# A two-layer decoder step: sample states and head sums in array quarters, first gather moved ahead

## The chip, the cores and the metric

One core of a Trainium2 chip runs the whole kernel; the other cores are not used. The metric is the device time of one execution in microseconds, lower is better, given as the median of several runs.

## What is computed

One inference step of a two-layer decoder, for a prompt of 256 tokens and 8 samples of 4 tokens, so 288 token columns, with D = 1024, all in fp32. Layer 0 is sparse attention beside a short convolution and a dense feed-forward block. Layer 1 is RWKV-7 time mixing with 16 heads of 64, and then a mixture of 8 experts of which each token takes 2. The change touches only layer 1. Three parts of it matter here:

```python
kk = heads(k * k_k)
kk = kk * lax.rsqrt(jnp.maximum(jnp.sum(kk * kk, axis=-1, keepdims=True), 1e-24))   # per token and head

def step(S, inp):                      # S: 64 x 64 per head; output wkv_sample is S after the 4 tokens
    r_t, w_t, k_t, v_t, kk_t, a_t = inp
    sa = jnp.einsum('bhvk,bhk->bhv', S, -kk_t)
    S = S * w_t[:, :, None, :] + sa[..., None] * (kk_t * a_t)[:, :, None, :] + v_t[..., None] * k_t[:, :, None, :]
    return S, jnp.einsum('bhvk,bhk->bhv', S, r_t)

for e in range(N_EXPERTS):             # top-2 of 8, combine holds the two gates of a token
    out = out + combine[..., e:e + 1] * swiglu(x, w_gate[e], w_up[e], w_down[e])
```

The per-head sum of squares over 64 channels, its inverse root, and that factor laid back over the 64 channels of each head are the "head sums" and the "spreading". The "new states of the sample" are the 16 heads x 8 samples of S after the 4 tokens.

## The kernel before, in words

The five engines run five instruction streams written by hand, tied by semaphores; the order of work is the order of the code in each stream. SP (SyncE) issues nearly all loads of weights and most of the outputs. A matmul in fp32 is two instructions on TensorE, and each has its weight load, so counts in the profile are twice those of the code. The channels of a token lie on partitions, 128 to a chunk, eight chunks (index c or hp), two heads to a chunk (index par, partitions 0 to 63 and 64 to 127).

**Time mixing, the factors.** TensorE runs 48 projection jobs of 16 instructions (`krv_job`, through the helper on line 774), each [128 x 128] weights against 288 columns. Between them stand small jobs. After job 32 it waits for ScalarE's squares `sqk` and sums them by head (line 1156): eight accumulating matmuls with a [128 x 16] slice of the constant `head_rows`, one per chunk, into 16 partitions of bank 0. Then jobs 33 to 35, during which VectorE clamps the sums (line 2353), ScalarE takes the root (line 1864), VectorE inverts and negates (lines 2355, 2356); GpSimd forms the decayed keys at the same time (lines 2883, 2884), and waits for the sums too before it does. Then TensorE spreads the 16 rows `rn` over all channels (line 1165): eight matmuls with [16 x 128] slices of `spread16`, into six banks in turn, so that the seventh and eighth wait for VectorE's products of line 2359 to free a bank. Then jobs 36 to 38, then the cross products of line 1175, which wait for VectorE's lines 2359 to 2367. `spread16` is laid out once by GpSimd (line 2871) behind the copies of the last rows. VectorE's stream before that: the token mixes (line 2327, in sets of eight), two small vectors (2332, 2333), the decay scale, the running sums and exponentials, the factor `kf` (line 2345), on which GpSimd waits to start its products of line 2877 and 2878, one pair per chunk as projections come. ScalarE squares them four chunks at a time.

**New states of the sample.** For each chunk hp, `new_state(hp)` on TensorE waits until GpSimd has decayed the old state `Ss`, and then turns the eight samples' 64 x 64 blocks with the identity, for both heads (line 1461, 16 matmuls, so 32 instructions), and adds `Zs` times `BKm`, 512 columns per head (line 1465, 4 instructions). Head par reads partitions of half par, and writes half par of its own bank (`K_BANKS[hp][par]`). ScalarE copies each head's half of 64 x 512 back to `Ss` (line 1982), and SP writes it out with one transfer per head (line 716). States 0 to 3 are made during the group norm of the mixing output, state 4 after the router's logits are turned, states 5, 6 and 7 after the rank sums (line 1554) that place each token in its experts. States 6 and 7 use the banks of states 4 and 5 and wait for their copies.

On ScalarE, `new_state(1)` stands between the squares of the group norm (line 1970) and its root (line 1976), on which VectorE (2549) and GpSimd (2922) wait, and then TensorE's transposes of y (1482).

**Experts.** `Ss` lies in the memory of the third of three weight buffers (`part2`, over the old ring). SP loads 16 pieces of 704 KB (gate and up of expert 0) ahead, then makes sure that all new states have been written out (`ws_out`), reads the number of blocks, and enters a loop with the pieces from 16 on: each waits until TensorE has used the piece that it replaces. A block is at most 96 tokens for each expert. TensorE reads the number of blocks, waits for the copy of state 7, and enters its loop: `gather()` picks the block's tokens of expert 0 by matmul (line 1573, 72 instructions into banks 0 and 1), VectorE turns them into `xe` (2649) and applies the gain (2654), then the eight experts follow: gate, up, gate (line 1607, columns in four quarters of the array), down (1624), up, the gather of the next expert, down. After the last expert it scatters the block (1591). Gate uses banks 0 to 2, up 3 to 5, down 6 and 7. The selection in `pick` for expert 0 is made by VectorE (2642) right after the ranks and before the rest of its preamble, which ends at line 2765.

**Names.** `half_(i)` is partitions 64i to 64i+63. `turned_s(engine, name)` waits for the copies of that name. `bk[i]` is PSUM bank i, 128 partitions x 512 columns.

## Time and profile before

| | |
|---|---|
| Median of 3 runs | 1519.91 us |
| Lowest, highest | 1518.69, 1524.91 us |
| The profiled execution's own time | 1520.28 us |
| Its span in the trace | 1518.5 us |
| TensorE matmul busy | 1451.0 us, 96% |
| VectorE, ScalarE, GpSimd busy | 457.5, 223.0, 165.6 us |
| HBM traffic | 375.59 MB read, 6.73 MB written, 252 GB/s over the span |
| Time-mixing layer | about 470 to 768 us |
| Router, states 4 to 7, gather | about 768 to 788 us |
| Experts | 787.8 to about 1503 us |

Times inside the trace count from the start of the span; between the span and the execution's own time lie 1.8 us. The span is the same whatever an engine's share of busy time is, so the chain of waits tells more than the shares. On the chain, "issue" is time in which the engine waited for nothing that the profile shows. PEclk in the windows is the granted TensorE clock as a share of 2.4 GHz.

### The profile page before, as it was taken

What the parts mean: (1) busy time and instruction counts of PE and PEld (TensorE: products, weight loads), DVE (VectorE), ACT (ScalarE), POOL (GpSimd) and SP (SyncE); (2) the same over time, 40 slices, a digit from 0 to 9 for tenths busy, and PEclk for the clock granted to TensorE, in tenths of its full rate; (3) what the DMA queues carried; (4) which work ended last, traced back from release to release, by engine and by line L of the source; (5) the groups of instructions that cost most, each with busy time, mean ns of one, the idle gap of its engine ahead of it and who ended that gap; (6) DMA issues with size and microseconds to landing.
All of it is one profiled execution on the core that took longest, in us unless ns stands there. A gap on an engine that the chain in (4) does not pass through costs nothing.

```text
span 1518.5 us, 39153 instructions
## 1 busy us (share of the span) xinstructions
PE 1451.0 (96%) x17792; PEld 936.8 (62%) x17792; DVE 457.5 (30%) x983; ACT 223.0 (15%) x485; POOL 165.6 (11%) x208
## 2 busy tenths in 40 slices
PE   6989989999999999987989999999999999999996
PEld 4767877777777777776644545555454555545453
DVE  2399331111024557774331110212111021211123
ACT  3144120000003412233120000000000000000001
POOL 4237200000000315125100000000000000000100
PEclk9999999999999999998999999999999999999999
DMA  9745034444534420305579999999999999999995
GB/s 287 219 139 153 14 113 145 133 135 143 162 104 116 132 84 3 59 3 143 191 276 414 413 411 412 374 413 369 414 385 396 414 369 413 373 412 386 394 403 217
DMA packets 187551, 384.86 MB, mean 253 GB/s; under 512 B 42463, under 2 KB 125631, under 8 KB 187258
## 3 DMA queue, kind: packets, MB, share of 16 engines
q1 hardware_dynamic: 180352, 365.84, 65.5%
q0 software_dynamic: 3616, 12.85, 2.2%
q10 hardware_dynamic: 3418, 3.68, 0.7%
q8 instruction: 140, 2.29, 0.6%
q14 instruction: 25, 0.20, 0.0%
HBM read 375.59 MB, written 6.73 MB: 252 GB/s over the span
## 4 chain that ended last, share of the span: by engine, by line
PE 88%; DVE 8%; DMA 1%; ACT 1%; issue 1%; SPq 0%; POOL 0%; DVEq 0%; ACTq 0%
PE bk L1607 30%; PE bk L1624 15%; PE bk L1089 11%; PE bk L774 9%; PE bk L1102 6%; PE bk L1526 2%; PE bk L1573 2%; PE bk L1004 2%; PE bk L1195 1%; DMA ring<-in_w_in_even 1%; DVE left L2184 1%; DVE tops L2182 1%; PE bk L1117 1%; PE bk L1138 1%; DVE sc_p L2169 1%
## 5 line engine op out<-in xcount | busy, mean ns | idle before, releaser
L1607 PE MATMUL bk<-part,xe 128*32 128x352 f32 x6144 | 459.1, 460 | 2.3 <-DVE xe L2654 2.3
L1607 PEld LDWEIGHTS bk<-part,xe 128*32 128x32 f32 x6144 | 207.8, 110 | 248.3 <-issue 245.9
L1624 PE MATMUL bk<-part,hidT 128*32 128x256 f32 x4224 | 231.4, 379 | 1.2 <-DVE hidT L2693 1.2
L1624 PEld LDWEIGHTS bk<-part,hidT 128*32 128x32 f32 x4224 | 141.9, 110 | 88.7 <-issue 2.6
L2689 DVE TENSOR_TENSOR hp<-sg,bk 128x352 f32<-128x352 f32 x48 | 37.6, 784 | 468.1 <-PE bk L1607 468.1
L1089 PE MATMUL bk<-xn,ring 128*128 128x288 f32 x704 | 173.8, 410 | 3.3 <-DMA ring<-in_ffn_up 3.3
L1089 PEld LDWEIGHTS bk<-xn,ring 128*128 128x128 f32 x704 | 135.4, 192 | 41.3 <-issue 3.5
L774 PE MATMUL bk<-mx,ring 128*128 128x288 f32 x384 | 98.1, 415 | 0.0
L774 PE MATMUL bk<-xg,ring 128*128 128x288 f32 x336 | 88.3, 422 | 8.2 <-DMA ring<-in_w_in_even 6.6
L774 PEld LDWEIGHTS bk<-mx,ring 128*128 128x128 f32 x384 | 73.2, 193 | 21.4 <-issue 1.2
L1102 PE MATMUL bk<-hid,ring 128*128 128x288 f32 x352 | 85.5, 406 | 0.0
L774 PEld LDWEIGHTS bk<-xg,ring 128*128 128x128 f32 x336 | 65.2, 197 | 27.7 <-issue 7.3
L1102 PEld LDWEIGHTS bk<-hid,ring 128*128 128x128 f32 x352 | 66.9, 190 | 18.5
L2942 POOL TENSOR_TENSOR free_now<-row_ss 128x1 f32 x5 | 1.0, 193 | 668.2 <-DMA expert_rows<-ye 650.3
L2042 ACT COPY ye<-bk 32x256 f32<-32x256 f32 x48 | 17.4, 363 | 368.4 <-PE bk L1624 367.8
L2035 ACT ACTIVATE sg<-bk 128x352 f32<-128x352 f32 x48 | 22.3, 464 | 313.3 <-PE bk L1607 309.3
L2716 DVE COPY ye<-bk 32x256 f32<-32x256 f32 x48 | 20.3, 422 | 99.0 <-PE bk L1624 98.3
L2268 DVE TENSOR_TENSOR gs<-bk,rs 128x288 f32<-128x288 f32 x22 | 10.1, 458 | 128.6 <-PE bk L1089 128.6
L1526 PE MATMUL bk<-gT,ro 128*128 128x288 f32 x128 | 34.5, 427 | 0.0
L2864 POOL MEMSET rmask<- 128x288 f32 x1 | 0.5, 496 | 311.4 <-DVE xg L2276 311.4
L1573 PE MATMUL bk<-xr,pick 128*32 128x256 f32 x576 | 32.6, 379 | 1.5 <-ACT Ss L1982 1.5
L1813 ACT ACTIVATE sg<-gs 128x288 f32<-128x288 f32 x22 | 9.8, 444 | 151.9 <-DVE gs L2268 151.9
(535 smaller groups left out, 1298.3 us busy)
## 6 DMA issues: line engine op xcount, KB each, us to landing
part<-in_moe_gate SPq DMA_DIRECT2D x136, 704.0 KB, 7.2
part<-in_moe_up SPq DMA_DIRECT2D x136, 704.0 KB, 8.6
part<-in_moe_down SPq DMA_DIRECT2D x128, 704.0 KB, 8.5
ring<-in_rwkv_w_rkv SPq DMA_DIRECT2D x24, 512.0 KB, 4.0
ring<-in_ffn_gate SPq DMA_DIRECT2D x22, 512.0 KB, 6.0
ring<-in_ffn_up SPq DMA_DIRECT2D x22, 512.0 KB, 5.2
ring<-in_ffn_down SPq DMA_DIRECT2D x22, 512.0 KB, 4.6
ring<-in_w_in_even SPq DMA_DIRECT2D x16, 512.0 KB, 6.9
```

Of the source, the lines that this page charges most:

```text
L774: last = mm(out, w[:, k], rhs[:, k], start=k == 0, stop=k == KC - 1)
L1004: last = nc.tensor.matmul(bk[4 + c // 2][:, TP * (c % 2):TP * (c % 2) + TP], w[:, k], mixT[:, k, 0:TP], start=k == 0 and c % 2 == 0, stop= ...
L1089: last = mm(bk[2 * m + f % 2][:, 0:T], slots[2 * m + k // 4][:, k % 4, (f % 2) * P:(f % 2 + 1) * P], xn1[:, k], start=k == 0, stop=k == KC ...
L1102: last = mm(bk[banks[c]][:, 0:T], w[:, f % 2, c * P:(c + 1) * P], hid[:, f], start=f == 0, stop=f == FC - 1)
L1526: last = mm(bk[OUT_BANK(c)][:, 0:T], w[:, k], gT[:, k], start=k == 0, stop=k == KC - 1)
L1573: last = mm(gate_bk[g // 2][32 * q:32 * q + 32, 256 * (g % 2):256 * (g % 2) + 256], pick[:, i, 32 * g:32 * g + 32], in_parts[:, q], start= ...
L1607: last = mm(banks[g][32 * c:32 * c + 32, 0:FQ], xe[:, k, 32 * g:32 * g + 32], parts[ph % 3][:, FH * k + FQ * c:FH * k + FQ * c + FQ], star ...
L1624: last = mm(down_bk[g // 2][32 * q:32 * q + 32, 256 * (g % 2):256 * (g % 2) + 256], hidT[:, half, g, 32 * m:32 * m + 32], parts[ph % 3][:, ...
L2035: nc.scalar.activation(sg2[:, g], gate_bk[g][:, 0:FQ], ACT.Silu).then_inc(silu_ok, 1)
L2042: last = nc.scalar.copy(ye[32 * g:32 * g + 32, 256 * q:256 * q + 256], down_bk[g // 2][32 * q:32 * q + 32, 256 * (g % 2):256 * (g % 2) + 256])
L2689: V.tensor_tensor(hp[:, g].rearrange("p (m j) -> p j m", m=NM), sg2[:, g].rearrange("p (j m) -> p j m", m=NM), up_bk[g][:, 0:FQ].rearrange ...
L2716: last = V.tensor_copy(ye[32 * g:32 * g + 32, 256 * q:256 * q + 256], down_bk[g // 2][32 * q:32 * q + 32, 256 * (g % 2):256 * (g % 2) + 256])
```

## The change

Three things are done.

1. **Head sums and spreading.** The sums of chunks 0 to 3 go to four column quarters of the array (32 columns each, partitions 32(c%4) and up of bank 0), and chunks 4 to 7 accumulate into the same four. `head_rows` is 34 wide, and its slice of 32 puts the two heads of a chunk on rows 12 and 13 (c < 4) or 14 and 15 of the quarter. `rn` has 128 rows. The spreading reads the quarter's 32 rows with a new table `head_of`, made by VectorE in four copies behind the mixes of set 4; GpSimd's `spread16` is gone.
2. **New states in four quarters.** Even samples are written to half par and odd ones to the other half; bank `K_BANKS[hp][0]` holds the even ones of both heads and `K_BANKS[hp][1]` the odd ones, 256 columns each. The wide product becomes four of 256 columns. ScalarE copies 128 x 256 per bank. SP writes four transfers of 64 KB per state.
3. **The first gather.** TensorE reads the block count after state 5, gathers, makes states 6 and 7, and enters the loop. The gather that opened the loop's body now closes it. The wait for state 7's copy stands before the first up product.

```diff
-    c["head_rows"] = np.arange(30)[None, :] == 14 + (p // HD)[:, None]
+    c["head_rows"] = np.arange(34)[None, :] == 14 + (p // HD)[:, None]
...
-    rn = sbt("rn", [RH, T], at=starts["rs"])
-    spread16 = sbt("spread16", [RH, D], at=starts["cst"] + 4 * COL["sin"][0])
+    rn = sbt("rn", [P, T], at=starts["rs"])
+    head_of = sbt("head_of", [P, 2, 2, HD], at=starts["cst"] + 4 * COL["sin"][0])
+    quarter = lambda c: slice(32 * (c % 4), 32 * (c % 4) + 32)
+    HALF_NB = NB // 2 * HD
...
             turned_s(sp, f"K{hp}")
+            by_parity = O["wkv_sample"][0].rearrange("(j o) h v k -> o h v j k", o=2)
             for par in range(2):
-                sp.dma_start(O["wkv_sample"][0, :, 2 * hp + par].rearrange("b v k -> v b k"),
-                             Ss[half_(par), hp].rearrange("p (b k) -> p b k", b=NB)).then_inc(ws_out, 16)
+                for odd in range(2):
+                    rows = Ss[half_(par ^ odd), hp, HALF_NB * odd:HALF_NB * odd + HALF_NB]
+                    sp.dma_start(by_parity[odd, 2 * hp + par], rows.rearrange("p (j k) -> p j k", k=HD)).then_inc(ws_out, 16)
...
-        sp.wait_ge(ws_out, 16 * RH)
+        sp.wait_ge(ws_out, 32 * RH)
...
-            last = mm(bk[0][0:RH, 0:T], C["head_rows"][:, 14 - 2 * c:30 - 2 * c], sqk[:, c], start=c == 0, stop=c == KC - 1)
+            at = 2 - 2 * (c // 4)
+            last = mm(bk[0][quarter(c), 0:T], C["head_rows"][:, at:at + 32], sqk[:, c], start=c < 4, stop=c >= 4)
...
-            mm(bk[c % 6][:, 0:T], spread16[:, P * c:P * c + P], rn[:],
+            mm(bk[c % 6][:, 0:T], head_of[quarter(c), c // 4].rearrange("p a v -> p (a v)"), rn[quarter(c)],
...
             for b in range(NB):
+                odd, at = b % 2, b // 2 * HD
                 for par in range(2):
                     r = half_(par)
-                    mm(bk[K_BANKS[hp][par]][r, b * HD:(b + 1) * HD], Ss[r, hp, HD * b:HD * b + HD], C["ident64"][r],
-                       start=b == 0, stop=False, skip_group_check=True)
-            for par in range(2):
-                r = half_(par)
-                last = mm(bk[K_BANKS[hp][par]][r, :], Zs[r, hp], BKm[r, hp].rearrange("p b k -> p (b k)"),
-                          start=False, stop=True, skip_group_check=True)
+                    mm(bk[K_BANKS[hp][odd]][half_(par ^ odd), at:at + HD], Ss[r, hp, HD * b:HD * b + HD], C["ident64"][r],
+                       start=b < 2, stop=False, skip_group_check=True)
+            for odd in range(2):
+                for par in range(2):
+                    r = half_(par)
+                    last = mm(bk[K_BANKS[hp][odd]][half_(par ^ odd), 0:HALF_NB], Zs[r, hp],
+                              BKm[r, hp].rearrange("p (j o) k -> p o j k", o=2)[:, odd],
+                              start=False, stop=True, skip_group_check=True)
...
         new_state(5)
-        for hp in (6, 7):
-            turned_s(pe, f"K{hp - 2}")
-            new_state(hp)
...
                 if k == 0 and e == 0:
+                    turned_s(pe, "K7")
                     pe.wait_ge(sc_ok, blk * 6 + 6)
...
-        turned_s(pe, "K7")
         pe.wait_ge(lg_mm, KC + 1)
+        pe.wait_ge(pick_ok, 1)
+        gather()
+        for hp in (6, 7):
+            turned_s(pe, f"K{hp - 2}")
+            new_state(hp)
         with pe.Fori(0, n_blocks) as blk:
-            pe.wait_ge(pick_ok, blk * NE + 1)
-            gather()
             for e in range(NE):
                 expert(blk, e)
             for g in range(6):
                 scatter(blk, g)
+            gather()
...
-            for par in range(2):
-                last = nc.scalar.copy(Ss[half_(par), hp], bk[K_BANKS[hp][par]][half_(par), :])
+            for odd in range(2):
+                last = nc.scalar.copy(Ss[:, hp, HALF_NB * odd:HALF_NB * odd + HALF_NB], bk[K_BANKS[hp][odd]][:, 0:HALF_NB])
...
         mixed(4, 0)
+        for c in range(4):
+            r = quarter(c)
+            V.tensor_copy(head_of[r].rearrange("p h a v -> p (h a) v"),
+                          C["ident"][r, 32 * c + 12:32 * c + 16].unsqueeze(2).broadcast_to([32, 4, HD]))
...
-        V.tensor_scalar(rn[:], bk[0][0:RH, 0:T], 1.0e-24, None, ALU.max).then_inc(nk_ok, 1)
+        V.tensor_scalar(rn[:], bk[0][:, 0:T], 1.0e-24, None, ALU.max).then_inc(nk_ok, 1)
...
-        G_.tensor_copy(spread16[:].rearrange("p (h v) -> p h v", h=RH),
-                       C["ident"][0:RH, 0:RH].unsqueeze(2).broadcast_to([RH, RH, HD])).then_inc(mask_ok, 1)
```

## Rows read from the trace of the kernel before

**Rows 1.** The page's part 4, the chain that ended last, by engine

```profile
PE 88%; DVE 8%; DMA 1%; ACT 1%; issue 1%; SPq 0%; POOL 0%; DVEq 0%; ACTq 0%
```

**Rows 2.** The chain in order of time (start us, us, what), time-mixing layer

```profile
535.01 3.98 PE bk L1156 x16
539.00 11.84 PE bk L774 x48
550.84 5.56 PE bk L1165 x16
556.40 13.68 PE bk L774 x48
```

**Rows 3.** Windows (busy us and instructions by engine, PEclk, DMA share, GB/s)

```profile
535.00:539.00 4.00, 4.00 (x18) 1.48 (x17) 0.47 (x2) 1.73 (x3) 0.00 (x0) 1.00 0.44 131
...
553.30:556.30 3.00, 3.00 (x7) 1.66 (x5) 1.52 (x4) 0.00 (x0) 0.00 (x0) 0.50 0.19 55
556.40:560.10 3.70, 3.70 (x8) 2.70 (x9) 3.63 (x4) 0.00 (x0) 0.00 (x0) 0.50 0.00 0
...
788.90:792.20 3.30, 3.30 (x28) 1.21 (x24) 0.00 (x0) 0.00 (x0) 0.00 (x0) 0.50 1.00 415
```

**Rows 4.** The chain in order of time, state 5 and experts

```profile
774.18 1.08 PE bk L1461 x32
775.26 0.86 PE bk L1465 x4
...
787.78 44.50 PE bk L1607 x576
```

**Rows 5.** Timeline (start, us, engine, line, operation, [idle before <-releaser])

```profile
717.22 1.17 ACT L1982 COPY Ss<-bk 64x512 f32<-64x512 f32 x2
...
779.80 0.14 DVE L2765 COPY blocks_f<-blocks_f 1x1 f32<-1x1 f32 x1
779.99 1.17 ACT L1982 COPY Ss<-bk 64x512 f32<-64x512 f32 x2 [0.86 <-PE bk L1465]
...
781.39 3.62 PEld L1573 LDWEIGHTS bk<-xr,pick 128*32 128x32 f32 x72 [2.33 <-issue]
...
785.55 1.11 DVE L2649 STREAM_TRANSPOSE xe<-bk 128x256 f32<-128x256 f32 x3 [5.60 <-PE bk L1573]
```

**Rows 6.** Timeline of VectorE, time-mixing layer

```profile
541.97 2.53 DVE L2356 TENSOR_SCALAR rn<-rn 16x288 f32<-16x288 f32 x1
...
551.55 2.46 DVE L2359 TENSOR_TENSOR t<-t,bk 128x288 f32<-128x288 f32 x5 [7.05 <-PE bk L1165]
...
556.93 2.29 DVE L2362 TENSOR_TENSOR AR<-t,cumx 128x2048 f32<-128x2048 f32 x1
...
562.40 2.29 DVE L2367 TENSOR_TENSOR BK<-aT,cum 128x2048 f32<-128x2048 f32 x1
```

**Rows 7.** Groups by form on TensorE (busy us, mean ns, idle before)

```profile
L1573 PE MATMUL bk<-xr,pick 128*32 128x256 f32 x576 | 32.6, 379 | 1.5 <-ACT Ss L1982 1.5
...
L1015 PE MATMUL bk<-sc,cst 32*128 32x256 f32 x16 | 1.4, 426 | 0.0
```

**Rows 8.** Timeline of GpSimd, factors

```profile
523.91 1.00 POOL L2877 TENSOR_SCALAR t<-kT,vecT 128x288 f32<-128x288 f32 x1 [0.25 <-ACT kT L1838]
```

**Rows 9.** Groups by form on ScalarE, 530 to 790

```profile
L1919 ACT COPY BKs<-bk 64x256 f32<-64x256 f32 x4 | 1.5, 365 | 0.3 <-PE bk L1227 0.3
```

**Rows 10.** Timeline of TensorE, level products

```profile
580.04 1.16 PE L1195 MATMUL bk<-Y,Cj 64*64 64x64 f32 x64 [1.84 <-DVE Y L2385]
```

**Rows 11.** The line of the output transfers (ns min/median/max, first and last start)

```profile
L716 SPq DMA_DIRECT2D out_wkv_sample<-Ss x16: 595/632/1308, 715.6 to 781.8; - x16
```

**Rows 12.** DMA issues by line (KB each, median us to landing)

```profile
out_wkv_sample<-Ss SPq DMA_DIRECT2D x16, 128.0 KB, 2.5
```

**Rows 13.** Timeline of SP, first experts

```profile
785.34 3.94 SPq L736 DMA_DIRECT2D part<-in_moe_gate  x8
```

**Rows 14.** Timeline of TensorE, the end

```profile
1503.00 4.63 PE L1591 MATMUL bk<-ye,giveT 96*32 96x512 f32 x36 [1.49 <-DVE ye L2716]
```

More of the change, by code:

```diff
@@ L296, in build @@
     rmask = sbt("rmask", [P, T], at=starts["cst"] + 4 * COL["cos"][0])
-    rn = sbt("rn", [RH, T], at=starts["rs"])
-    spread16 = sbt("spread16", [RH, D], at=starts["cst"] + 4 * COL["sin"][0])
-    assert COL["sin"][0] + D <= COL["delta_mask"][0]
+    rn = sbt("rn", [P, T], at=starts["rs"])
+    head_of = sbt("head_of", [P, 2, 2, HD], at=starts["cst"] + 4 * COL["sin"][0])
+    assert COL["sin"][0] + 4 * HD <= COL["delta_mask"][0]
+    quarter = lambda c: slice(32 * (c % 4), 32 * (c % 4) + 32)
     Sp = sbt("Sp", [P, 2, KC, HD])
@@ L1160, in _ @@
         pe.wait_ge(rn_ok, 1)
-        pe.wait_ge(mask_ok, 2)
         for c in range(KC):
```

## The prediction, made before the kernel was run

> **What bounds the kernel now.** I read the page's chain first: almost nine tenths of the span is TensorE work [rows 1], so an edit pays only where it shortens TensorE's own queue or removes what that queue waits for. Then I read the chain in order of time at the two places that the diff touches. In the time-mixing layer it runs on TensorE without a break through the head sums, 48 projection matmuls, the spreading and 48 more projection matmuls [rows 2]; nothing else is late there. Two things stand out. The head sums and the spreading are single matmuls one after another over 16 columns or 16 rows of the array. And the second 48 projection matmuls take 13.68 us where the first 48 take 11.84: the windows show why, a granted clock of 0.50 (1.2 of 2.4 GHz) from about 553.3 to 560.1 us, which began while TensorE was in the spreading [rows 3]. The head sums before it left the clock at full speed. At the second place the chain goes through states 5, 6 and 7, then the gather, then the first expert [rows 4, 5]; between them TensorE stands idle twice, first for ScalarE's copy of state 7, then, from 785.5 to 787.78, for VectorE's transposes of the gathered columns [rows 5]. Another half-speed stretch lies right behind that second pause, 788.9 to 792.2 [rows 3]. From there on the expert stage is TensorE at a fixed pace to the end.
>
> **Head sums.** Before: 16 instructions (two per fp32 matmul), 3.98 us [rows 2], 0.25 us each. After: the same number, but eight matmuls with 32 columns each in four column quarters. The nearest row is the expert product, also 128x32 in four column quarters, 576 in 44.50 us [rows 4], 77 ns each for 352 moving columns; for 288 that is 63 ns, so 16 take 1.0, with the last one's drain 1.1 us. Gain 2.9 (bounds: 0 if the quarters don't overlap, 3.0). The 32-row result costs the engines behind it nothing new: they work per partition on the same 288 columns. Their answer now comes 2.9 earlier; before it was ready at 544.5 (VectorE's last step, stretched to 2.53 us [rows 6]) and was used at 550.8, so over 6 us of projections cover it before and after.
>
> **Spreading.** Before: 5.56 us [rows 2], of which 3.0 at half clock. After: each matmul has 32 rows and 128 columns, four row quarters at once into four banks. The nearest row is the selection's spreading, the same 32x128 form in four row quarters and four banks: 16 instructions of 256 columns busy for 1.4 us [rows 7]; one after another at 0.25 x 256/288 each they would be 3.6, so they overlap. The first four matmuls then take about 0.6 us. Six banks serve eight results, so matmuls 6 and 7 wait for VectorE's products 0 and 1, 0.49 us apiece [rows 6]: first product at +0.7, second done at +1.7, last matmul done at +2.3. Gain 5.56-2.3 = 3.3 (bounds: 1.6 if nothing overlaps but the clock stays up, 4.7 if VectorE held nothing back). VectorE becomes the slower one here: eight products end at +4.6, that is at 547.9+4.6 = 552.5 instead of 556.9. Its following work took from 556.93 to 564.69 [rows 6], so it is done at 560.3. The matmuls that need it come after 48 projections: 547.9+2.3+11.84 = 562.0. So TensorE stays the bound with 1.7 us in hand; if that is gone, VectorE's chain is late next.
>
> **The clock there.** The array read 16 of 128 rows for the stretch before the clock fell. After the change the quarters read all 128 and the light stretch is 2.3 us with projections on both sides, so I take the fall as gone: the 48 projections run 11.84 instead of 13.68, gain 1.8 (bounds 0 and 1.8). The first part of the layer gives 2.9+3.3+1.8 = 8.0 us.
>
> **What pays for it.** VectorE gets four copies of 32x256 behind the second set of mixes. A product of 288 elements a partition takes it 0.49 us [rows 6], so they are 2.0 at most, and exponentials, factors and GpSimd's products start that much later. GpSimd already waits 0.25 us for ScalarE's copy of a projection before its sixth pair at 523.91 [rows 8], and each pair takes 1.8 where a projection takes 3.9, so it has caught up a pair later, some 7 us before the head sums. I cost it at nothing; without that cover it is 2.0. GpSimd loses its one copy, off the path: nothing.
>
> **States 0 to 3** lie in the group norm, where TensorE waits. ScalarE's two copies of state 1 (1.17 us, 64x512 [rows 5]) stand between the squares and the root of the path. They become two of 128x256; a 256-column copy takes 0.365 [rows 9], so 0.73: gain 0.4 (bounds 0.4 and -1.3: TensorE finishes these states sooner, idles longer, and its clock could fall before the transposes of y).
>
> **States 4 to 7 and the gather.** A state now costs 1.08+0.86 = 1.94 us [rows 4]: 32 instructions on two of the four 64x64 quarters, then four of 512 columns. After: the 32 go round all four; 64 such instructions take 1.16 us on four quarters [rows 10], so 0.6; the wide products become eight of 256 columns over four, half of 0.86 plus a drain, 0.5. About 1.1 a state. The order becomes: state 5, the read of the block count, gather, states 6 and 7, loop. State 5 starts at 774.18 as before (it follows the rank sums, which wait for ScalarE) and ends at 775.3. The read of the count was under ScalarE's copy before and is bare now; the trace does not show it alone. It is between nothing and the 2.3 us from TensorE's last weight load to the gather's first [rows 5]; I take 0.9, since that gap also held the copy's second half and its signal. Gather at 776.2, 4.16 us until VectorE takes it, then 2.23 until the expert starts, as before [rows 4, 5]: 782.6. TensorE's states 6 and 7 end at 780.4+2.2 = 782.6, entering the loop adds perhaps 0.3. VectorE's own preamble ended at 779.94 [rows 5], so it is there in time, or 0.6 late if entering its loop costs it a microsecond. Expert 0 starts at 783.1 against 787.78: gain 4.7 (bounds 3.3 and 5.6). The wait for state 7's copy now stands before the second product of expert 0, 14 us later: nothing.
>
> With the idle 2.3 us gone I take the half-speed stretch behind it as gone too: half of 3.3 us [rows 3], gain 1.7 (bounds 0 and 1.7).
>
> **Queues and the end.** SP issues 16 output transfers for these four states instead of eight, and weights 16 and up wait for all. At 0.63 us per issue [rows 11] state 7's four go out from 783.5 to 786; they land 2.5 later, weights from about 789 instead of 785.34 [rows 12, 13]. Expert 0 first needs them after two thirds of the 44.50 us row, 783.1+29.7 = 812.8. Slack shrinks by 8 us and stays above 15: nothing. The loop's closing gather runs once for no one, as the 576 instructions of rows 7 are eight gathers of 72, so one block; it starts when TensorE's last work ends, 1507.6 [rows 14], and takes 4.1 (8.2 at half clock), with the span going on to 1518.5: nothing.
>
> **Sum:** 8.0+0.4+4.7+1.7 = 14.8 us off the profiled execution's 1520.3 is 1505.5. The median of the three runs shown is 0.4 below that execution; I leave the forecast at 1505.5. A measurement here tells about 0.5% (7.6 us) from no change.
>
> **Rivals.** (a) The clock gives nothing: both stretches stay, or others appear, since what precedes each shifts by some us. 1505.5+1.8+1.7 = 1509. For: the work before the first expert still has two short pauses. Against: the head sums did not bring it down. 0.20. (b) VectorE or a bare wait is late next: its chain misses 562.0 by a few us, or count read and loop entry take the full 2.3: together up to 5 us, 1510. 0.12. (c) The state products don't overlap fourfold, because both row halves now write the same bank at once, where before each had its own. Then states 6 and 7 stay 1.94 each, the expert starts at 784.6, and the time is 1507. Against: the level products of rows 10 are on four quarters with both row halves in one bank, and take 18 ns each against 34 for the state's. 0.05. The Trainium skill (TensorEngine Tiling (Array Packing), Gotcha 1: PSUM Pressure) says row tiles can't access one bank simultaneously; by that rule (c) would hold, and the trace's row disagrees. (d) Quarters don't overlap in the head sums and the spreading and the clock still falls: that part gives nothing, 1513.5, no change. Against: rows 4 and 7. 0.05. (e) Slower: the outputs' transfers hold up the weights. If each of the 16 costs SP D us, the loads start at 775+16D+2.5 and land 4 later; TensorE stalls once D exceeds 2.0, and the time passes 1528 once D exceeds 3.4, since a stalled expert stage regains nothing. Against: 0.63 per issue now. 0.03. The Trainium skill (DMA: Bandwidth & Descriptors, Rules for kernel authors) has transfers below 64 KB pay mostly overhead; these go from 128 KB [rows 12] to 64, and no row of before shows one of that size here.
>
> **Chances.** Forecast 0.55, its own range 1502 to 1508.5. Faster by over 0.5% (below 1512.3): 0.55+0.20+0.12+0.05, less what of (b) spills over, 0.90. Same 0.07, slower 0.03. The range 1501.5 to 1512.5 takes in (a) to (c) and a clock that rises elsewhere.
>
> **What would show it.** Head sums near 1.1 us, spreading near 2.3, clock 1.00 through 545 to 562, the cross products at 562; a state's 32 instructions in 0.6 us; the gather near 768 and expert 0 near 775 on the shifted axis; no SP wait in the expert stage that TensorE has to wait for. Wrong if TensorE waits for VectorE before the cross products, or if a half-speed stretch stands at a new place on the chain.

## The result and the profile after

| | before | after |
|---|---|---|
| Median | 1521.20 us (4 runs) | 1512.01 us (4 runs) |
| Lowest to highest | 1518.69 to 1524.91 | 1510.52 to 1516.85 |
| Profiled execution, its span | 1520.28, 1518.5 | 1516.85, 1515.0 |

The ratio is 0.9941, with a 95% interval from 0.9924 to 0.9958: 9.2 us faster, where 14.8 were forecast. The profiled execution of after was its slowest of four, so its span hides part of the gain, and I ran the same kernel again below (`changed_again`) for a second trace.

Line numbers below the edits move: L1156 is now L1161, L1165 is L1170, L774 is L778, L1461 is L1467, L1573 is L1578, L1607 is L1612, L716 is L721.

The page's part 4 (the chain by engine) and part 2 (the granted clock in 40 slices) of after, against [rows 1]:

```profile
PEclk9899999999999999998899999999999999999999
...
PE 88%; DVE 8%; DMA 1%; issue 1%; ACT 1%; SPq 0%; DVEq 0%
```

The bound is the same. The page alone doesn't show the change: the places have to be read one by one. The chain in order of time, against [rows 2]:

```profile
539.20 1.11 PE bk L1161 x16
540.30 11.84 PE bk L778 x48
552.14 0.73 PE bk L1170 x8
552.87 0.45 DVE t L2372
553.32 0.04 issue
553.36 1.11 PE bk L1170 x4
554.47 11.84 PE bk L778 x48
566.31 2.02 PE bk L1180 x128
...
578.73 1.99 PE bk L1200 x64
580.72 6.05 PE bk L778 x16
586.77 2.02 PE bk L1200 x128
588.79 4.08 PE bk L778 x16
```

From the head sums to the cross products it takes 566.31 - 539.20 = 27.1 us; in [rows 2] it is 535.01 to 570.08, 35.1. The one step on VectorE is the wait of matmul 6 for its bank. But two things are new: the head sums start 4.2 us later than before, in front of which no work was changed on TensorE; and 12 us behind the cross products, 64 level products take 1.99 us where [rows 10] has 1.16, and 16 projection instructions take 6.05 where the next 16 take 4.08. The windows of after (columns as in [rows 3]) name the cause, and two more such places:

```profile
578.20:585.00 6.80, 6.27 (x74) 4.95 (x75) 6.68 (x8) 1.45 (x3) 0.00 (x0) 0.52 0.01 2
...
721.60:731.80 10.20, 10.20 (x32) 6.63 (x33) 8.07 (x19) 1.50 (x3) 5.66 (x6) 0.52 0.32 66
776.00:783.00 7.00, 6.19 (x65) 3.32 (x65) 4.28 (x37) 1.46 (x6) 0.00 (x0) 0.53 0.38 78
```

The granted clock is about half (1.2 of 2.4 GHz) at each. The second stretch begins behind the pause before the transposes of y, the third in the new gather. The timeline of the second place in the changed kernel, columns as in [rows 5], shows the group norm:

```profile
716.78 0.65 PE L1472 MATMUL bk<-BKm,Zs 64*64 64x256 f32 x8
717.44 0.63 ACT L1991 COPY Ss<-bk 128x256 f32<-128x256 f32 x2
...
718.55 1.90 POOL L2934 TENSOR_TENSOR y_rows<-y_rows,gst 128x1024 f32<-128x1024 f32 x1 [6.48 <-DVE gst L2562]
...
721.11 0.39 PE L1490 MATMUL bk<-cst,y_rows 128*128 128x128 f32 x1 [3.68 <-DVE y_rows L2567]
```

ScalarE's copies of state 1 take 0.63 us where two of [rows 5] took 1.17, and TensorE stands still for 3.68 us behind state 3, where it stood still for 2.35 us before. And TensorE's timeline at the gather, against [rows 4, 5]:

```profile
774.90 0.69 PE L1467 MATMUL bk<-cst,Ss 64*64 64x64 f32 x32
775.42 0.71 PE L1472 MATMUL bk<-BKm,Zs 64*64 64x256 f32 x8
776.93 6.88 PE L1578 MATMUL bk<-xr,pick 128*32 128x256 f32 x72 [0.81 <-DVE pick L2655]
783.75 0.69 PE L1467 MATMUL bk<-cst,Ss 64*64 64x64 f32 x32
784.26 0.61 PE L1472 MATMUL bk<-BKm,Zs 64*64 64x256 f32 x8
784.70 0.64 PE L1467 MATMUL bk<-cst,Ss 64*64 64x64 f32 x32
785.16 0.61 PE L1472 MATMUL bk<-BKm,Zs 64*64 64x256 f32 x8
786.12 4.32 PE L1612 MATMUL bk<-part,xe 128*32 128x352 f32 x53 [0.35 <-DVE xe L2667]
```

States 6 and 7 now lie under VectorE's transposes, and the two idle pauses are gone but for 0.81 and 0.35 us. The gather itself takes 6.9 us instead of 4.13.

The next table cuts the span of each trace at the same seven places, to show where the time went. The stretches are cut at the first instruction of a line on TensorE; in brackets stands the time lost to a low clock, (1 - PEclk) times the length of the window, in us. For the first expert to the scatter, 715 us long, PEclk is rounded to 1.00 in each; the 1.7 is from the half-speed stretch of 3.3 us in [rows 3].

| stretch | before | after | changed_again |
|---|---|---|---|
| start to head sums | 534.9 | 539.1 | 535.7 |
| head sums to cross products | 35.1 (3.5) | 27.1 (0) | 27.1 (0) |
| cross products to transposes of y | 151.6 (4.5) | 154.9 (10.8) | 153.7 (9.2) |
| transposes of y | 5.5 (1.6) | 6.9 (3.4) | 6.7 (3.1) |
| output projection to rank sums | 45.6 (1.8) | 45.5 (1.8) | 45.7 (1.8) |
| rank sums to first expert | 15.1 (0) | 12.6 (3.4) | 11.0 (1.8) |
| first expert to scatter | 715.2 (1.7) | 713.5 (0) | 713.5 (0) |
| scatter to end | 15.5 | 15.4 | 15.4 |

So 8.0 came from the head sums, 2.5 to 4.1 from the path to the experts, 1.7 behind the first expert; 3.3 (or 2.1) and 1.4 (or 1.2) were given back in the two middle stretches, and 4.2 (or 0.8) ahead of the change. The runs had to tell what of this is the change's doing.

### The profile page after: what moved, and what is told of

Read it like the earlier page. It is cut to its first block, busy times and chain, and to the rows that moved or that the text cites. A ratio compares the mean times of both kernels' runs of the same rounds, so it can differ in the third digit from the quotient of the medians.

```text
span 1515.0 us, 39378 instructions
## 1 busy us (share of the span) xinstructions
PE 1451.6 (96%) x17896; PEld 940.7 (62%) x17896; DVE 456.6 (30%) x987; ACT 218.7 (14%) x485; POOL 164.2 (11%) x207
## 3 DMA queue, kind: packets, MB, share of 16 engines
q10 hardware_dynamic: 3418, 3.68, 0.7%
## 4 chain that ended last, share of the span: by engine, by line
PE 88%; DVE 8%; DMA 1%; issue 1%; ACT 1%; SPq 0%; DVEq 0%
PE bk L1612 30%; PE bk L1629 15%; PE bk L1093 11%; PE bk L778 9%; PE bk L1106 6%; PE bk L1578 2%; PE bk L1534 2%; PE bk L1008 2%; PE bk L1200 1%; DMA ring<-in_w_in_even 1%; DVE left L2193 1%; DVE tops L2191 1%; PE bk L1121 1%; PE bk L1142 1%; DVE sc_p L2178 1%
## 5 line engine op out<-in xcount | busy, mean ns | idle before, releaser
L1612 PE MATMUL bk<-part,xe 128*32 128x352 f32 x6144 | 457.4, 459 | 0.3 <-DVE xe L2667 0.3
L1612 PEld LDWEIGHTS bk<-part,xe 128*32 128x32 f32 x6144 | 207.3, 110 | 245.1 <-issue 242.7
L778 PE MATMUL bk<-xg,ring 128*128 128x288 f32 x336 | 90.3, 429 | 9.0 <-DMA ring<-in_w_in_even 8.9
L778 PE MATMUL bk<-mx,ring 128*128 128x288 f32 x384 | 98.2, 415 | 0.0
L778 PEld LDWEIGHTS bk<-mx,ring 128*128 128x128 f32 x384 | 73.2, 193 | 21.2 <-issue 0.9
L778 PEld LDWEIGHTS bk<-xg,ring 128*128 128x128 f32 x336 | 66.7, 201 | 29.0 <-issue 9.6
L1578 PE MATMUL bk<-xr,pick 128*32 128x256 f32 x648 | 40.3, 400 | 0.8 <-DVE pick L2655 0.8
L1578 PEld LDWEIGHTS bk<-xr,pick 128*32 128x32 f32 x648 | 23.5, 116 | 17.0 <-issue 6.2
## 6 DMA issues: line engine op xcount, KB each, us to landing
part<-in_moe_down SPq DMA_DIRECT2D x128, 704.0 KB, 14.8
```

Source lines behind the costliest of these rows:

```text
L778: last = mm(out, w[:, k], rhs[:, k], start=k == 0, stop=k == KC - 1)
L1578: last = mm(gate_bk[g // 2][32 * q:32 * q + 32, 256 * (g % 2):256 * (g % 2) + 256], pick[:, i, 32 * g:32 * g + 32], in_parts[:, q], start= ...
L1612: last = mm(banks[g][32 * c:32 * c + 32, 0:FQ], xe[:, k, 32 * g:32 * g + 32], parts[ph % 3][:, FH * k + FQ * c:FH * k + FQ * c + FQ], star ...
```

## The experiments

Twelve runs, in three rounds. Beside each round the kernel before was run too: medians 1521.88 (27 runs), 1523.31 (17) and 1520.95 us (11). Ratios are to it.

### One part at a time

`heads_only`, `states_only` and `gather_only` are the kernel before with one numbered part of the change each; their diffs are the hunks of `head_rows`/`rn`/`head_of`, of `new_state`, and of `gather()` with `turned_s(pe, "K7")`, as printed above.

> Head sums and spreading in quarters alone, on the kernel before. Clock theory (each part saves the work that was forecast, and part of it is given back because TensorE idles between smaller pieces and its clock falls at new places): the stretch from the head sums to the cross products is 27.1 us as in the changed kernel instead of 35.1, and a fall of the clock in the level products costs 0 to 3: 5 to 8 us faster than before. Rival (the parts' gains overlap, and the 9 us come from this part alone): 9 us faster. Rival (the gain of this part is swallowed by VectorE's chain further on): under 3 us faster.

Measured: 1518.08 us, ratio 0.9970 [0.9954, 0.9985]. The chain:

```profile
538.02 1.11 PE bk L1158 x16
...
565.14 2.02 PE bk L1177 x128
```

27.1 us again, 8.0 less than before, but the median gained only 3.8 us, less than the 5 to 8 expected. The stretch starts at 538.0, 3.1 later than before, much as in after (more on that below), and where it is 33.5 in the old code the gain is 6.4 (`gather_only`).

> New states in four quarters alone, on the kernel before. Clock theory: a state's 32 instructions in 0.56 us and its wide ones in 0.5, the path from state 5 to the first expert 13.6 us before becomes about 10.4 (three states shorter by 0.85, the last copy by 0.5), and the group norm gives 0.5; with a clock fall at the first expert as before, 3 us faster; with a new one in the router or the gather, 0 to 2. Rival (SP's 32 transfers delay the expert weights): TensorE waits for pieces of the third buffer in expert 0.

Measured: 1519.87 us, 0.9989 [0.9975, 1.0003]. From the rank sums to the first expert 13.3 us instead of 15.1, and the two pauses remain. The clock fell while TensorE made states 5 and 6: their 32 instructions took 1.14 and 1.09 us there, those of state 7 at full clock 0.65. The transposes of y take 6.2 (2.5 lost to the clock) instead of 5.5. Behind the first expert there is no half-speed stretch (713.5 us to the scatter), although the order of gather and states is the old one.

> First gather ahead of states 6 and 7 alone, on the kernel before. Clock theory: states still 1.9 us each, so states 6 and 7 take 3.9 us behind the gather and end 1.7 us after the gathered columns are ready: the path from state 5 to the first expert becomes about 10.8 us instead of 13.6, 2.8 faster at full clock, 0 to 1 faster if the clock falls in the gather. Rival (the closing gather costs time at the end): the span behind the last scatter is longer than before by up to 4 us.

Measured: 1517.06 us, 0.9969 [0.9956, 0.9982]. The median is 4.8 us below the kernel before's, where 2.8 were expected. From the rank sums to the first expert 11.1 us, at full clock, with the old states of 1.94 us each. That is as short as in `changed_again`, which lost 1.8 us to the clock there. That chain ends so:

```profile
785.56 0.86 PE bk L1465 x4
786.42 42.74 PE bk L1604 x576
```

VectorE has `xe` ready at 785.60, and TensorE starts the expert 0.8 us later, when it is through with state 7. In the full change `xe` ends last (785.99, and the expert starts at 786.12). So the quartering does shorten this path, by some 0.6 us at full clock (10.5 in `fill_both` below), and the clock, which fell on this path in nearly all traces of quartered states, took that back. The first expert's half-speed stretch is gone in this kernel too (713.5). But it is also missing in `before_wide` below, which is the kernel before with one wider table:

```profile
790.60:1504.10 713.50, 710.76 (x10875) 366.46 (x10876) 109.23 (x204) 38.55 (x94) 6.62 (x11) 1.00 0.99 397
```

Of the four traces with the old order it stands in two (before and `heads_only`, 715.2) and not in the other two (`before_wide` and `states_only`). So the 1.7 us of the table are not shown to be the change's doing. The first stretch of `gather_only` is of old code only:

```profile
535.00 3.98 PE bk L1156 x16
538.99 11.84 PE bk L774 x48
550.83 4.07 PE bk L1165 x16
554.90 13.53 PE bk L774 x48
```

The spreading took 4.07 here and 5.56 in [rows 2]: in that code the clock falls each time (all four traces with it), but not at the same moment, so this stretch is 33.5 or about 35. In before and `states_only` it fell inside the spreading. In `gather_only` and `before_wide` it stayed up through the spreading and fell about 1 us behind it (in `gather_only` 0.99 from 554 to 556 us and 0.50 from 556 to 559), and less time was lost. Measured from 33.5 the gain of the new code is 6.4. The windows of the next stretch, cross products to transposes of y, follow for three kernels, none of which changes a line on TensorE there, one fence per kernel: before, `gather_only`, `heads_only`.

```profile
570.00:721.60 151.60, 131.85 (x3754) 111.61 (x3753) 100.75 (x166) 48.28 (x96) 53.48 (x39) 0.97 0.23 52
```

```profile
568.40:724.00 155.60, 136.28 (x3753) 115.42 (x3752) 100.72 (x166) 48.18 (x96) 53.51 (x39) 0.93 0.23 51
```

```profile
565.10:716.70 151.60, 130.06 (x3753) 110.16 (x3753) 100.68 (x166) 48.19 (x96) 53.47 (x39) 0.98 0.23 52
```

151.6 us at a clock of 0.97 or 0.98, 155.6 at 0.93: the length of this stretch goes with the clock of the execution, and it is long and short in old code alike. The execution that my sum was made against was one of the short ones. The product of the three ratios is 0.9928; the whole change has 0.9941 and 0.9947. No interaction shows beyond the intervals.

### Is the idle time what the clock answers to?

A filler is a matmul of the identity against `xT` into a bank that is free, whose result nothing reads. It does no work of the kernel; it only keeps TensorE running in a pause.

`fill_levels`: in front of the first level products, where TensorE waits for VectorE twice, 1.84 and 1.30 us, between 574.4 and 578.7 in after. The added wait is for a result that is long there, and keeps the filler behind the last use of its bank.

```diff
             for p2 in range(2):
+                if j == 1:
+                    pe.wait_ge(job_ok, NIN + 39)
+                    fill(6, 3 - p2)
                 pe.wait_ge(y_ok, 2 * (j - 1) + p2 + 1)
```

> The changed kernel with idle matmuls in the two pauses in front of the first level products only (three and two, 128x128 against 288 columns). Clock theory: no half-speed stretch in the level products, 1.5 to 3 us faster than the changed kernel in the median. Rival: as the changed kernel, 1512, or up to 0.5 slower for the fillers.

Measured: 1509.93 us, 0.9917 [0.9890, 0.9944]. The stretch took 151.2 us, 3.0 lost to the clock.

`fill_both` adds two fillers behind state 4 and one before the gather.

```diff
         new_state(4)
+        fill(7, 2)
         pe.wait_ge(sel2_ok, 1)
...
         pe.wait_ge(lg_mm, KC + 1)
+        fill(2, 1)
         pe.wait_ge(pick_ok, 1)
```

> The changed kernel with idle matmuls of 128x128 against 288 columns, whose results nothing reads, in TensorE's pauses: three and two in front of the first two level products, two in front of the rank sums, one in front of the first gather. Clock theory: the clock stays at 1.00 through the level products and the gather; level products and the projection behind them 2.8 us shorter, gather 4.2 instead of 6.9, so 4 to 6 us faster than the changed kernel where its clock fell at both. Rival (the clock has no part in it): no faster than the changed kernel, or slower by what the fillers outlast the pauses (up to 1 us).

Measured: 1510.07 us, 0.9923 [0.9903, 0.9943]. 152.1 us in the middle stretch, 7.6 lost. From the rank sums to the first expert 10.5, with no fall:

```profile
768.00:795.00 27.00, 25.12 (x422) 13.33 (x424) 11.66 (x72) 9.21 (x23) 1.60 (x2) 1.00 0.43 129
```

These are shorter than after's, but 151.2 and 152.1 lie at or near the short end of what unfilled kernels showed (151.6 to 155.6), so the lengths alone don't show what the fillers did. `all_gaps` below tells more by place. At the gather the clock does tell. In the nine other traces with quartered states the clock fell between the rank sums and the first expert (1.7 to 3.4 us lost), whether or not the gather had been moved; in the four with the old states it did not. This is the only kernel with quartered states in which it stayed at 1.00 there, and its gather took 4.1 us. It is one trace, and it gained little time: kernels with the change and without these fillers needed 10.5 to 12.6 us for this path. The fillers themselves cost some: the gather starts 3.8 us behind the first rank sum, and 3.3 in `changed_again`.

`fill_y` fills the pause before the transposes of y with five matmuls.

```diff
         turned_s(pe, "K0")
         new_state(3)
+        turned_s(pe, "K1")
+        fill(4, 5)
```

> The changed kernel with five idle matmuls behind state 3, in TensorE's pause before the transposes of y. Clock theory: with the quartered states TensorE ends them sooner, idles longer, and its clock falls one stretch earlier; with the pause filled the transposes run at full clock, from the first transpose of y to the first output projection 4.5 to 5 us instead of 6.5 to 6.9, and the half-speed stretch behind it is shorter or gone, up to 5 us in all. Rival (the transposes wait for VectorE and ScalarE, and the clock is set by what they themselves keep busy): 6.5 to 6.9 us as before, and the half-speed stretch stays.

Measured: 1509.95 us, 0.9937 [0.9920, 0.9954]. The window of the transposes, of `fill_y` first and then of `changed_again`, which ran on the same chip:

```profile
717.80:722.60 4.80, 4.58 (x24) 3.02 (x25) 3.84 (x8) 1.18 (x3) 1.82 (x3) 1.00 0.48 100
```

```profile
716.50:723.20 6.70, 6.70 (x25) 4.09 (x26) 4.91 (x10) 1.11 (x3) 2.54 (x4) 0.53 0.48 99
```

4.8 us at clock 1.00 against 6.7 at 0.53, and the output projection behind it 44.9 instead of 45.7. The fall goes with the pause. Filled, in `fill_y` and in `all_gaps`, it is gone; in every profile with quartered states and an empty pause of 3.5 to 4.0 us it is there (6.2 to 6.9 us), and with the old, longer states and a pause of 1.3 to 2.4 us it is milder (5.2 to 5.6). The output projection alone says less (it took 44.7 to 46.1 in kernels without this filler), but the two stretches together, from the transposes to the rank sums, took 49.6 and 49.7 us with it and 50.9 to 52.5 in the twelve other traces.

`states_in_gaps` uses real work instead: state 5 goes before the rank sums and state 6 ahead of the gather.

```diff
         new_state(4)
+        new_state(5)
         pe.wait_ge(sel2_ok, 1)
...
-        new_state(5)
+        turned_s(pe, "K4")
+        new_state(6)
...
-        for hp in (6, 7):
-            turned_s(pe, f"K{hp - 2}")
-            new_state(hp)
+        turned_s(pe, "K5")
+        new_state(7)
```

> The changed kernel with the same states at other places: state 5 in front of the rank sums, state 6 in front of the gather, state 7 alone behind it, so that TensorE's two pauses there hold work. Clock theory: no fall of the clock in the gather, which takes 4.2 us instead of 6.9; first expert 2 to 3 us nearer to the rank sums than in the changed kernel, 2 to 3 us faster in the median. Rival (the clock has no part, the gather waits for the picks): no faster, since the picks and the transposes set the time either way.

Measured: 1510.3 us, 0.9912 [0.9886, 0.9939]. From the rank sums to the first expert 11.0 us, 1.8 lost to the clock, as in `changed_again` without the move: a miss. The states in the pauses did not keep the clock up, and the interval overlaps the change's own.

### The late start of the head sums

Kernels with the new head sums start them at 535.7 to 542.0 us, with the old ones at 534.9 to 536.3. The change makes the table of constants four columns wider (`head_rows`), and that table is loaded at the start. `same_width` takes the four columns off another constant in the changed kernel, `before_wide` gives the kernel before the wider one.

```diff
-    c["slots"] = np.tile(np.arange(P)[None], (P, 1))
+    c["slots"] = np.tile(np.arange(P - 4)[None], (P, 1))
```

```diff
-    c["head_rows"] = np.arange(30)[None, :] == 14 + (p // HD)[:, None]
+    c["head_rows"] = np.arange(34)[None, :] == 14 + (p // HD)[:, None]
```

> The changed kernel with the last constant four columns narrower (its last four are never read), so that the table of constants is 2942 wide again and every tile behind it lies where it lay in the kernel before. In the three profiles of kernels with the wider table the head sums start at 538.0 to 542.0 us, in the three with the old width at 534.9 to 536.3. Layout theory (the 16 bytes more per row, or the 32-byte shift of the tiles, slow the first loads): head sums start at 535 to 537 and the median is 3 us below the changed kernel's, some 1509. Rival (chance: the first loads vary by themselves): head sums anywhere from 534 to 542, median as the changed kernel's, about 1512.

> The kernel before with head_rows 34 columns wide instead of 30, nothing else: the opposite edit. Layout theory: 3 us slower than before, head sums start at 538 or later. Rival (chance): no difference from before within 1.5 us.

Measured: `same_width` 1512.36 us, 0.9917 [0.9893, 0.9941], head sums at 540.1; `before_wide` 1524.24 us, 1.0002 [0.9987, 1.0017], head sums at 535.7. The width is not it. The traces say where the time lies, though not why. The first matmul of line 1008 (1004 before), in layer 0, starts at 164.3 us in before and at 168.5 in after, and from there to the head sums it takes 370.6 us in both. In the fourteen traces that first matmul starts between 164.3 and 171.4 us, and the rest takes 369.5 to 370.8. So all of the lateness arises ahead of that matmul and of every changed instruction (VectorE's four copies start at 504.67 in after), and those copies cost the path nothing. What varies there is open. `before_wide` also gave a third trace of old code in the middle stretch, nearly as slow as `gather_only`:

```profile
569.20:724.20 155.00, 136.44 (x3753) 115.55 (x3752) 100.88 (x166) 48.20 (x96) 53.47 (x39) 0.93 0.23 51
```

### Rows or length: what brought the clock down in the spreading

The old spreading differs from the new in two ways: it reads 16 rows of the array, and it runs 4 to 5.6 us instead of 2.3. `spread_128_rows` is the changed kernel with the eight matmuls one after another again, but over all 128 rows.

```diff
-    head_of = sbt("head_of", [P, 2, 2, HD], at=starts["cst"] + 4 * COL["sin"][0])
+    head_of = sbt("head_of", [P, KC, 2, HD], at=starts["cst"] + 4 * COL["sin"][0])
...
-            mm(bk[c % 6][:, 0:T], head_of[quarter(c), c // 4].rearrange("p a v -> p (a v)"), rn[quarter(c)],
+            mm(bk[c % 6][:, 0:T], head_of[:, c].rearrange("p a v -> p (a v)"), rn[:],
...
-        for c in range(4):
-            r = quarter(c)
-            V.tensor_copy(head_of[r].rearrange("p h a v -> p (h a) v"),
-                          C["ident"][r, 32 * c + 12:32 * c + 16].unsqueeze(2).broadcast_to([32, 4, HD]))
+        for c in range(KC):
+            row = 32 * (c % 4) + 12 + 2 * (c // 4)
+            V.tensor_copy(head_of[:, c], C["ident"][:, row:row + 2].unsqueeze(2).broadcast_to([P, 2, HD]))
```

> The changed kernel, but the spreading reads all 128 rows in eight matmuls one after another, with a table that is zero outside a chunk's two rows, instead of 32 rows in quarters. Rows theory (the old spreading let the clock fall because it read 16 of 128 rows, not because of its length): 16 instructions at 0.24 us, 3.9 to 4.3 us instead of 2.3, at full clock, and the projections behind it 11.8: head sums to cross products 28.8 to 29.2, 1.7 to 2 us slower than the changed kernel. Rival (its length, 4 us of matmuls with K small in number, let it fall): the clock falls in it, 33.5 to 35.1 less the 2.9 of the sums, so 30.6 or more.

Measured: 1512.75 us, 0.9947 [0.9934, 0.9960]; TensorE's timeline and the window over it:

```profile
550.79 4.04 PE L1170 MATMUL bk<-rn,head_of 128*128 128x288 f32 x16
554.67 11.80 PE L778 MATMUL bk<-mx,ring 128*128 128x288 f32 x48
```

```profile
545.00:562.00 17.00, 17.00 (x72) 13.32 (x71) 10.24 (x13) 1.20 (x3) 0.00 (x0) 1.00 0.39 113
```

The spreading is nearly as long as the old one in `gather_only` (3.88 us from its start to the next projection's, against 4.07), TensorE is as busy, and the clock stays at 1.00. So its length alone did not bring the clock down, and the 16 rows are what is left of the two. One thing more differs from the kernel before: the head sums ahead of it are in quarters here. The old head sums, over 128 rows and 16 columns, left the clock at 1.00 while they ran [rows 3], but whether they had a part in the fall behind them was not tested; that needs the new sums with the old spreading. The stretch takes 28.5 us. So the 8.0 us split into 2.9 for the quartered head sums (3.98 to 1.11), 28.5 - 27.1 = 1.4 for the quarters of the spreading, and 3.7 for the clock (2.1 counted from 33.5). Counted from the profiled execution the clock is the largest part, counted from 33.5 the head sums are.

### The change again, and the version with every pause filled

> The changed kernel itself once more, on the same chip as the three below, for a second profile and a direct comparison. Clock theory (a fall depends on where TensorE's pauses happen to lie, so it differs between executions of one program, while the work between stays the same): head sums to cross products 27.1 us again; from the cross products to the transposes of y either about 151.5 or about 155, and from the rank sums to the first expert between 9.8 and 12.6. Rival (the falls belong to the program): 154.9 and 12.6 as in the first profile.

Measured: 1512.36 us (1508.04 to 1515.51), 0.9947 [0.9929, 0.9965]; its profiled execution took 1510.65 us, span 1508.8, and is the third column of the table. The same program gave spans of 1515.0 and 1508.8: 3.4 of that difference lie in front of the head sums, 1.2 in the middle stretch and 1.6 on the path to the first expert, the last two where the clock differs. In the middle stretch both possibilities of the expectation missed: 153.7 lies between 151.5 and 155.

```profile
768.93 1.18 PE L1562 MATMUL bk<-sel,cst 128*128 128x8 f32 x12 [1.26 <-ACT bk L2023]
...
772.21 5.39 PE L1578 MATMUL bk<-xr,pick 128*32 128x256 f32 x72 [0.74 <-DVE pick L2655]
...
779.90 2.55 PE L1612 MATMUL bk<-part,xe 128*32 128x352 f32 x29 [0.35 <-DVE xe L2667]
```

`all_gaps` is the changed kernel with the edits of `fill_levels`, `fill_y` and `states_in_gaps` together.

> The changed kernel with states 5 and 6 in the pauses around the rank sums, idle matmuls in front of the first level products and five behind state 3: all three together. Clock theory: cross products to transposes of y 151.5, those to the first output projection 5, rank sums to first expert 10 to 11: 5 to 7 us faster than the changed kernel on this chip, some 1505. Rival (the falls move on to the next pause): under 2 us faster.

Measured: 1508.59 us (1505.83 to 1510.02), 0.9918 [0.9903, 0.9932], on the same chip as `changed_again`: 3.8 us below it and 12.4 below the kernel before. The two intervals just meet at 0.993, so it is likely faster than the change, but not certainly, and it stayed short of the 1505 expected. The windows of the middle stretch and of the transposes:

```profile
563.50:717.50 154.00, 136.96 (x3790) 116.48 (x3789) 101.06 (x167) 46.62 (x97) 53.50 (x39) 0.94 0.21 51
...
717.50:722.20 4.70, 4.52 (x25) 2.87 (x24) 3.38 (x7) 1.00 (x2) 1.82 (x3) 1.00 0.48 100
```

The filler before y worked again (4.7 us and 44.9 behind it). The middle stretch stayed long: 154.0 us at 0.94. But the fillers did not fail where they stand. A window over the level products of `all_gaps`:

```profile
573.00:592.00 19.00, 18.69 (x433) 14.75 (x432) 18.73 (x24) 5.00 (x10) 9.11 (x4) 1.00 0.01 3
```

The clock is at 1.00 there in all three kernels with these fillers. In the same window seven of the eleven others have 0.82, old code among them, and four have 1.00. Three against seven of eleven could still be chance, but it speaks for the fillers. What `all_gaps` lost, it lost from 114 to 152 us behind the cross products, where no filler stands. Before lost most of its 4.5 there too (113 to 124 us behind). What sets the falls there stays open.

## Why the prediction was right, and where its sum was too large

Faster was given 0.90, and it was faster. The measured median, 1512.0, lies in the wide range, 0.5 us from its upper end; it lies outside the forecast's own range (1502 to 1508.5, chance 0.55) and above what rivals (a) and (b) gave (1509 and 1510). The forecast was 6.5 us too low. By its own sign of being wrong, a half-speed stretch at a new place on the chain, the part on the clock came out wrong: such a stretch stands in the gather.

**Head sums, spreading, clock: right.** 1.11 against 1.1 us, 2.3 against 2.3, clock 1.00, together 8.0 against the same profiled execution. The reason given for the clock, 16 of 128 rows, fits `spread_128_rows`, with the open end named there. One size was off without harm: eight products of VectorE took 3.00 us and not 3.9, so its chain ended at 563.6 with 2.7 us in hand. The 8.0 is, however, what that one execution paid: of four traces of the same old code two had 35.0 and 35.1 and two 33.5, so the gain is 6.4 to 8.0.

**VectorE's four copies: right.** 1.17 us for all four, and GpSimd has caught up with the projections well ahead of the head sums (it waits 1.83 us for ScalarE before its seventh pair, at 531.97).

**Group norm: the step that failed.** Its gain was 0.8 and not 0.4 (from the end of VectorE's centring, line 2551, to the start of GpSimd's product, line 2934, 2.11 us instead of 2.88), but the end that I had written as a bound and not taken, the clock lower at the transposes of y, is what happened in each kernel with quartered states: 6.2 to 6.9 us instead of 5.2 to 5.6. `fill_y` shows that it goes with the pause, which had grown from 2.35 to 3.68 us. The transposes cost 1.2 to 1.4 more, so with its 0.8 the step loses about 0.5 instead of giving 0.4.

**States 5 to 7 and the gather: mechanism right, size too large.** 4.7 was forecast; 2.5 and 4.1 came out in the two traces of the change. The state products take 0.69 us for 32 (0.51 until the wide ones start) against 0.6, the wide ones 0.61 against 0.5. The block count read, for which I put 0.9, does not show: the pause before the gather is 0.81 in all, and part of it goes to VectorE's `pick`, by which the trace has it end. What was missing is the clock: the gather takes 5.4 or 6.9 us instead of 4.13. Without that the sum holds: by the forecast it took 10.4 us from the rank sums to the first expert, and `fill_both`, at full clock, took 10.5. The ordering alone gives 4.0 of it (`gather_only`, 11.1), the shorter states the other 0.6, which the clock took back.

**The stretch behind the first expert: right by luck.** It is gone, as forecast (1.7). But `before_wide` and `states_only`, with the old order and the idle 2.3 us still in front of the expert, don't have it either, so the reason given is not shown. With quartered states a stretch of like size or more stands in the gather, and rival (a), which had other stretches appear, is half true.

**The rest.** SP's sixteen transfers take 0.62 us each, spread with their waits over 15.55 us, and the weights came at 793.40 instead of 789:

```profile
775.28 15.55 SPq L721 DMA_DIRECT2D out_wkv_sample<-Ss  x16
793.40 4.22 SPq L740 DMA_DIRECT2D part<-in_moe_gate  x8
```

No expert waits for a DMA (the page has 0.3 us before L1612, for `xe`), so rival (e) fell and the cost was nothing, as said. The four microseconds come from two things: states 6 and 7 follow a gather at half clock, so that ScalarE copies them only from 784.94 and 785.84, and their eight transfers then queue up on SP until 790.8. The closing gather runs from 1503.85 beside the scatter's tail, and from the scatter to the end it takes 15.4 instead of 15.5.

**The sum** was 14.8 against one execution and 9.2 by medians. The gather's term was 0.6 to 2.2 too large and the group norm's 0.9; that is 1.5 to 3.1. The head sums' 8.0 is up to 1.6 more than they usually give. The 1.7 behind the first expert is more than some executions of the old code had to give. The remainder lies mostly in the base: the profiled execution before had a short middle stretch (151.6; old code took 155.0 and 155.6 in two other traces, and the change took 154.9 and 153.7), so that I took as given what was luck, and the head sums start later in the new kernels (538.0 on the average of ten traces, 535.5 in four of the old). The first is shown by the traces. The second is not explained: it arises in layer 0, where nothing but the width of the constants was changed, and that is not it, so it may be chance.

**Rivals.** (b) fell: neither VectorE nor the bare wait is late. (c) fell: 32 state products on four quarters take 0.69 us instead of 1.10 to 1.15, with both row halves writing into one bank. The Trainium skill (TensorEngine Tiling (Array Packing), Gotcha 1: PSUM Pressure) says row tiles can't access one bank simultaneously; the trace disagrees, by this rate, for tiles that write different partitions. (d) fell by the 1.11 and 2.3.

## What to carry over

Make the sum of a forecast against more than one trace of the kernel before where the granted clock falls anywhere in it: one stretch took between 151.6 and 155.6 us with the same instructions on TensorE, and two traces of one program differed by 1.6 us on the path to the experts alone. A fall of the clock that the forecast removes may be absent from the old code in its next execution: look for it in a second trace before counting it. When work is shortened in front of a wait, the pause gets longer by as much, and the clock may take back more than was gained. Here a few matmuls that nothing reads, put into the pause before the transposes of y, made these 1.9 us shorter. And when an operation is moved in front of another, first ask which engine sets the start of what follows: here the move alone gave 4.0 us, and shortening the states behind it some 0.6 more, because VectorE then ended last.

## What was not expected of the hardware

- In all four traces with sixteen matmul instructions in a row over 16 rows of the array, the granted clock went to 0.50 during them or about 1 us behind them, with TensorE busy throughout. The same sixteen over 128 rows (3.88 us) left it at 1.00, and so did sixteen over 128 rows and 16 columns (3.98 us), each in the traces that have them.
- Which falls of the clock occur differs between traces of the same instructions on TensorE: the loss between the cross products and y was 4.5 us in before and 10.9 in `gather_only`. Two executions of one program, after and `changed_again`, lost 10.8 and 9.2.
- A transfer of half the size costs SP the same: 64 KB 617 ns to issue and 2.2 us to land, against 632 ns and 2.5 us for 128 KB [rows 11, 12].

```profile
L721 SPq DMA_DIRECT2D out_wkv_sample<-Ss x32: 595/617/1489, 715.7 to 790.2; - x32
...
DMA to landing us min/median/max: 2.1/2.2/3.0
```
